# Small matmuls of a fused two-layer kernel, issued inside weight units instead of between them

## The reference

```python
mod = silu(c) @ w_ada + b_ada
shift_m, scale_m, gate_m, shift_f, scale_f, gate_f = split(mod, 6)
h = rmsnorm(x, g_mix_pre) * (1 + scale_m) + shift_m
z = h @ w_in                       # q, k, v, fl (8 columns), pool, conv, three gates
log_f = log_sigmoid(fl + b_f); cum_f = cumsum(log_f)
logits = q @ k.T * scale + cum_f[query] - cum_f[key]   # 8 heads of 64, causal, softmax, @ v
merged = gate0 * (attn @ wa) + gate1 * (pool @ wb) + gate2 * (conv @ wc)
x = x + gate_m * rmsnorm(merged @ w_out, g_mix_post)
h2 = rmsnorm(x, g_ff_pre) * (1 + scale_f) + shift_f
x = x + gate_f * rmsnorm(square(relu(h2 @ w_ff1)) @ w_ff2, g_ff_post)
```

## Time and profile before

| | |
|---|---|
| median of 3 executions | 855.65 us (854.88 to 856.12) |
| profiled execution | 856.08 us |
| span of its profile | 854.7 us |
| PE busy | 801.0 us (94%) |
| DVE, ACT, POOL busy | 561.3, 416.5, 82.3 us |
| mean granted clock of TensorE | 0.974 of full |

### The profile page before, as it was taken

How to read it: one execution, slowest core, us unless ns; L and a number is a source line. 1 busy time by engine, 2 the same in 40 slices (tenths; PEclk the granted TensorE clock), 3 DMA queues, 4 the chain that set the end, 5 groups by cost and what they waited for, 6 DMA issues and landing times.

```text
span 854.7 us, 12953 instructions
## 1 busy us (share of the span) xinstructions
PE 801.0 (94%) x5264; PEld 728.8 (85%) x5264; DVE 561.3 (66%) x761; ACT 416.5 (49%) x610; POOL 82.3 (10%) x129
## 2 busy tenths in 40 slices
PE   2989999999969999999999999899987999999995
PEld 2889998999859999999989998688876999999994
DVE  4775887859965655656665889757444665555663
ACT  4445356653446454435456477447534644444341
POOL 6200960001110000000001000011000100000000
PEclk9998999999988999999999999999999999999998
DMA  9968777867644555555556554446434365565641
GB/s 306 351 220 293 260 261 255 290 230 260 210 135 131 190 189 181 187 183 179 191 178 192 174 151 149 144 152 201 141 99 123 124 197 183 187 191 183 194 148 50
DMA packets 83323, 163.70 MB, mean 192 GB/s; under 512 B 5424, under 2 KB 13808, under 8 KB 83264
## 3 DMA queue, kind: packets, MB, share of 16 engines
q1 hardware_dynamic: 81344, 157.31, 56.7%
q10 hardware_dynamic: 1424, 4.81, 1.7%
q0 software_dynamic: 496, 0.76, 0.3%
HBM read 161.81 MB, written 1.05 MB: 191 GB/s over the span
## 4 chain that ended last, share of the span: by engine, by line
PE 83%; ACT 7%; DVE 6%; issue 2%; POOL 1%; DMA 1%; SPq 0%; ACTq 0%; DVEq 0%; POOLq 0%
PE bank L1630 25%; PE bank L1631 25%; PE bank L1632 25%; ACT hi_ring L461 2%; DVE lo_ring L865 2%; PE bank L1784 1%; DVE ada_acc L897 1%; PE bank L1669 1%; PE bank L1689 1%; PE bank L2089 1%; DVE x_residual L971 1%; DMA ada_ring<-in_w_ada 1%; ACT gates L516 1%; PE bank L1798 1%; PE bank L1788 1%
## 5 line engine op out<-in xcount | busy, mean ns | idle before, releaser
L865 DVE TENSOR_TENSOR lo_ring<-raw_ring,hi_ring 128x1024 fp32r<-128x1024 f32 x248 | 304.9, 1234 | 209.0 <-ACT hi_ring L461 208.3
L461 ACT CAST hi_ring<-raw_ring 128x1024 fp32r<-128x1024 f32 x248 | 258.9, 1049 | 325.2 <-PE bank L1632 311.3
L1630 PE MATMUL bank<-h_hi,hi_ring 128*128 128x256 f32 x1008 | 292.5, 290 | 1.5 <-DVE h_lo L930 1.5
L1631 PE MATMUL bank<-h_lo,hi_ring 128*128 128x256 f32 x1008 | 289.2, 287 | 0.0
L1632 PE MATMUL bank<-h_hi,lo_ring 128*128 128x256 f32 x1008 | 289.0, 287 | 0.0
L1630 PEld LDWEIGHTS bank<-h_hi,hi_ring 128*128 128x128 f32 x1008 | 197.7, 196 | 4.8 <-issue 3.2
L1631 PEld LDWEIGHTS bank<-h_lo,hi_ring 128*128 128x128 f32 x1008 | 197.8, 196 | 0.8 <-issue 0.2
L1632 PEld LDWEIGHTS bank<-h_hi,lo_ring 128*128 128x128 f32 x1008 | 197.5, 196 | 0.0
L1630 PE MATMUL bank<-hi_ring,branch_hi 128*128 128x512 f32 x320 | 125.7, 393 | 2.8 <-DVE branch_lo L1009 2.7
L1631 PE MATMUL bank<-lo_ring,branch_hi 128*128 128x512 f32 x320 | 124.7, 390 | 0.0
L1632 PE MATMUL bank<-hi_ring,branch_lo 128*128 128x512 f32 x320 | 124.5, 389 | 0.0
(11 more groups left out here) (259 smaller groups left out, 937.3 us busy)
## 6 DMA issues: line engine op xcount, KB each, us to landing
raw_ring<-in_w_ff SPq DMA_DIRECT2D x128, 512.0 KB, 3.7
raw_ring<-in_w_in SPq DMA_DIRECT2D x64, 512.0 KB, 4.3
raw_ring<-in_w_out SPq DMA_DIRECT2D x16, 512.0 KB, 3.5
raw_ring<-in_w_xkv SPq DMA_DIRECT2D x16, 512.0 KB, 3.7
mem_v<-in_w_ada SPq DMA_DIRECT2D x12, 512.0 KB, 5.8
ada_ring<-in_w_ada SPq DMA_DIRECT2D x10, 512.0 KB, 4.9
mem_k<-in_w_ada SPq DMA_DIRECT2D x10, 512.0 KB, 5.3
raw_ring<-in_w_branch SPq DMA_DIRECT2D x8, 512.0 KB, 5.1
```

Of the source, the lines that this page charges most:

```text
L461: act.copy(m.hi[:, m.slot(u)], m.raw[:, m.slot(u)]).then_inc(s.hi_done, 1)
L865: dve.tensor_tensor(m.lo[:, m.slot(u)], m.raw[:, m.slot(u)], as_f32(m.hi[:, m.slot(u)]), ALU.subtract).then_inc(s.lo_done, 1)
L1630: pe.matmul(out, a_hi, b_hi, start=start, stop=False, skip_group_check=True)
L1631: pe.matmul(out, a_hi, b_lo, start=False, stop=False, skip_group_check=True)
```

## The change

Three pieces of small work move from the gap between two units into a unit: `unit_features` and `unit_tokens` get a function `beside`, called after each tile of three passes.

- The forget logits go from behind unit 14 into unit 15, two of the 16 matmuls after each of its eight tiles. Bank 0, into which they go, is wanted by unit 16.
- The scores of the first attention go from behind the unit of their step into that unit, one of the four parts after each second tile (first, third, fifth and seventh).
- The shift's columns go from behind unit (c = 4, j = 1) into the next unit, one matmul after each of eight tiles. The scale's columns go from ahead of unit 52 into it, two after each of its four tiles. Each column now counts up its semaphore, so the readers wait for 8. DVE reads the shift two units later, and the scale after its split of unit 56 instead of before it.

```diff
-                dve.wait_ge(s.ff_shift_ps, 1)
+                dve.wait_ge(s.ff_shift_ps, 8)
...
-            if c == 4 and j == 1:
+            if c == 4 and j == 3:
                 ada_columns(s.ff_shift_ps, s.ff_shift, 0, 8, 16, 24)
...
-    ada_columns(s.ff_cols_ps, s.ff_cols, 6, 8, 24, 32, G_FF)
     for n in range(2):
         for j in range(RING):
             if j == RING - 1:
                 post_scale(s.post1, n, OUT_BANKS[n], m.rows[:, 0, :])
+            if n == 0 and j == 1:
+                ada_columns(s.ff_cols_ps, s.ff_cols, 6, 8, 24, 32, G_FF)
...
                 mm = three_passes(bank[banks[f // 2]][:, (f % 2) * S:(f % 2) * S + S], m.hi[:, slot, k, fc],
                                   m.lo[:, slot, k, fc], x_hi[:, k0 + k, :], x_lo[:, k0 + k, :],
                                   first and k == 0 and f % 2 == 0, last and k == UK - 1)
+                if beside:
+                    beside(tiles * k + f)
...
-    def forget_logits():
-        pe.wait_ge(s.q_out, 2)
-        pe.wait_ge(s.small_in, SMALL_LOADS * DMA)
-        for tt in range(NT):
-            for k in range(KD):
-                mm = pe.matmul(bank[0][:, tt * NH:tt * NH + NH], m.h_f32[:, k, tt * P:tt * P + P], m.w_fl[:, k, :],
-                               start=(k == 0), stop=(k == KD - 1))
-        mm.then_inc(s.fl_ps, 1)
-        free[0] = s.fl_out, 1
+    def forget_logits(i):
+
+        if i == 0:
+            claim(0)
+            pe.wait_ge(s.small_in, SMALL_LOADS * DMA)
+        tt = i // 4
+        for k in (2 * (i % 4), 2 * (i % 4) + 1):
+            mm = pe.matmul(bank[0][:, tt * NH:tt * NH + NH], m.h_f32[:, k, tt * P:tt * P + P], m.w_fl[:, k, :],
+                           start=(k == 0), stop=(k == KD - 1), skip_group_check=True)
+        if i == 7:
+            mm.then_inc(s.fl_ps, 1)
+            free[0] = s.fl_out, 1
...
-                features(u, q, m.h_hi, m.h_lo, 2 * i)
-            if u == 14:
-                forget_logits()
+                features(u, q, m.h_hi, m.h_lo, 2 * i, beside=forget_logits if u == 15 else None)
...
+        def beside(i):
+            if i == 0:
                 claim(4, 5)
...
+            if i % 2 == 0:
+                score(s.att1, g, (4, 5), True, i // 2)
...
+    def ff_shift(i):
+        if i == 0:
+            claim(0)
+            pe.wait_ge(s.ada_used, 32)
+        ada_column(2, 0, i, s.ff_shift_ps)
+        if i == 7:
+            free[0] = s.ff_shift, 1
+
+    def ff_cols(i):
+        if i == 0:
+            claim(6)
+            pe.wait_ge(s.ada_used, 40)
+        ada_column(0, 6, 2 * i, s.ff_cols_ps)
+        ada_column(0, 6, 2 * i + 1, s.ff_cols_ps)
+        if i == 3:
+            free[6] = s.ff_cols, 1
```

More of the change, by code:

```diff
@@ L1632, in three_passes, with unit_features @@
         return pe.matmul(out, a_lo, b_hi, start=False, stop=stop, skip_group_check=True)
-    def unit_features(u, k0, x_hi, x_lo, banks, first, last, tiles=4):
+    def unit_features(u, k0, x_hi, x_lo, banks, first, last, tiles=4, beside=None):
         pe.wait_ge(s.lo_done, u + 1)
@@ L1643, in unit_features, with unit_tokens @@
                                   first and k == 0 and f % 2 == 0, last and k == UK - 1)
+                if beside:
+                    beside(tiles * k + f)
         return mm
-    def unit_tokens(u, k0, x_hi, x_lo, outs, first, last, cols=slice(0, UN), start_first=True):
+    def unit_tokens(u, k0, x_hi, x_lo, outs, first, last, cols=slice(0, UN), start_first=True, beside=None):
         pe.wait_ge(s.lo_done, u + 1)
@@ L1684, in turn_x, with ada_column @@
                 transposes(turn, m.x, tt, range(n * KD // 2, (n + 1) * KD // 2))
+    def ada_column(slot, b, i, done):
+        pe.matmul(bank[b][:, i:i + 1], m.ada_acc[:, slot + i // 4, i % 4 * P:i % 4 * P + P], m.ones[:, 0:1], start=True,
+                  stop=True, skip_group_check=True).then_inc(done, 1)
     def ada_columns(slot, slabs, b):
@@ L1771, in pe_program, with score, scores @@
             else:
-                features(u, q, m.h_hi, m.h_lo, 2 * i)
-            if u == 14:
-                forget_logits()
+                features(u, q, m.h_hi, m.h_lo, 2 * i, beside=forget_logits if u == 15 else None)
+            if u == 13:
+                free[0] = free[1] = s.q_out, 2
     free[5] = s.v_sum, 4
     free[2] = free[3] = s.k_out, 2
-    free[1] = s.q_out, 2
     free[6] = free[7] = s.mixA_out, 2
[L1780 to L1791, removed]
+    def score(a, g, banks, forget, i):
+        e, tt, c0, c1 = parts()[i]
+        rows = slice(64 * e, 64 * e + 64)
+        b = bank[banks[e]]
+        mm = pe.matmul(b[:, c0:c1], m.qT[rows, g, tt * P:tt * P + P], m.kT[rows, g, 0:c1 - c0], start=True,
+                       stop=not forget, skip_group_check=True)
+        if forget:
+            head = 2 * g + e
+            mm = pe.matmul(b[:, c0:c1], m.pick[0:2 * NH, head:head + 1].to_broadcast([2 * NH, P]),
+                           m.key_sums[0:2 * NH, 0:c1 - c0], start=False, stop=True, skip_group_check=True)
+        if i == 3:
+            mm.then_inc(a.scores.sem, 1)
+            free[banks[0]] = free[banks[1]] = a.logits.at(g + 1)
+    def scores(a, g, banks):
+        for i in range(4):
+            score(a, g, banks, False, i)
     def turn_prob(a, g, banks, soft):
@@ L1814, in attend, with scores1 @@
         free[b] = a.br.at(g + 1)
[L1816 to L1820, removed]
+    def scores1(step):
+        if step not in ATT1_AT:
+            return None
+        g = ATT1_AT.index(step)
+        def beside(i):
+            if i == 0:
                 claim(4, 5)
@@ L1826, in attention1 @@
                     pe.wait_ge(s.pick_ok, 1)
-                scores(s.att1, g, (4, 5), True)
+            if i % 2 == 0:
+                score(s.att1, g, (4, 5), True, i // 2)
+        return beside
+    def ff_shift(i):
[11 more added lines that the diff above has]
+        ada_column(0, 6, 2 * i + 1, s.ff_cols_ps)
+        if i == 3:
+            free[6] = s.ff_cols, 1
+    def attention1(step):
+        if step == 0:
+            cumulative()
+        for g, at in enumerate(ATT1_AT):
             if step == at + 4:
@@ L1836, in pe_program @@
     for j in range(RING):
-        features(MIX_B + j, j, m.h_hi, m.h_lo, 0)
+        features(MIX_B + j, j, m.h_hi, m.h_lo, 0, beside=scores1(j))
         attention1(j)
@@ L1845, in pe_program @@
             i = RING * c + j
-            features(GATES + i, j, m.h_hi, m.h_lo, b0)
+            features(GATES + i, j, m.h_hi, m.h_lo, b0,
+                     beside=ff_shift if (c, j) == (4, 2) else scores1(RING + i))
             attention1(RING + i)
@@ L1851, in pe_program @@
                 free[0], free[1] = (s.gate_row, 1), (s.gate_row, 3)
[L1852 to L1856, removed]
             if i == 13:
@@ L1889, in pe_program @@
             pe.wait_ge(s.merged_lo, j + 1)
-            tokens(OUT + RING * n + j, UK * j, m.h_hi, m.h_lo, b0, j == 0, j == RING - 1)
+            tokens(OUT + RING * n + j, UK * j, m.h_hi, m.h_lo, b0, j == 0, j == RING - 1,
+                   beside=ff_cols if n == 0 and j == 0 else None)
             if n == 1 and j == 1:
@@ L1972, in scores2 @@
             pe.wait_ge(s.k2_out, 2)
-        scores(s.att2, g, pair_banks(g), False)
+        scores(s.att2, g, pair_banks(g))
     def turn2(g):
```

16 lines of the change are left out of this document (7 added, 9 removed).

## The result

| | before | after |
|---|---|---|
| median | 856.12 us (5 executions, 854.88 to 858.39) | 864.72 us (5, 863.05 to 866.39) |
| ratio, 95% interval | | 1.0097 (1.0080 to 1.0115) |
| profiled execution, span | 856.08, 854.7 us | 865.01, 863.7 us |
| mean granted clock | 0.974 | 0.978 |
| DVE, ACT, POOL busy | 561.3, 416.5, 82.3 us | 562.6, 416.2, 82.2 us |

The change makes the kernel 8.6 us slower. The forecast was 4.2 us faster, the range ended at 855.0: both are wrong. The profiled executions differ by 8.9 us.

The account below looks back on a forecast made before the run. TensorE, on 83% of the chain of waits, was taken as the bound. Terms 2.5 + 4.5 - 2.3 + 0.1 - 0.6 = 4.2 us off 855.65 gave 851.4 us; range 848.9 to 855.0 (8 in 10).

Parts of the forecast that it names:

- the one on the shift's columns: 16 records inside a unit instead of ahead of it, DVE's read two units later: covered, priced at 0.
- Forget logits: Units 14 to 17: full clock saves 3.07 us, a new wait takes 0.55, net 2.5 us.
- the wait on L1089: Ahead of unit 16, TensorE waits for DVE to empty the forget logits' bank: some 0.5 us.
- The mixed unit: Rival, 13%: unit 15, 32 small records among 24 weight matmuls, still lowers the clock; 3.07 us stay, 854.5 us.
- Scores: First attention: three low stretches vanish, 4.5 us saved, against 2.3 us for 12 added changes between weight matmuls and scores.
- A boundary: Each change between weight matmuls and scores costs TensorE 0.19 us; three more per pair of heads.
- Scale's columns: At unit 52: full clock only brings TensorE 2 us early to a wait for `h_lo`; gain 0.1 us.
- The slower rival: Rival, 9%: the clock does not follow these runs or their grouping; nothing gained, 2.9 us added, 858.5 us.
- Another engine takes the gain: Rival, 10%: without low stretches, loads or DVE's splits may come late by 1 to 2 us; 853 us.
- the two waits for the probabilities unchanged: Sign of being right: TensorE's two waits for the probabilities, 1.1 us in all, stay as they are.
- Later restarts: Low stretches from 250.02 and 663.10: the clock may come back later, 0.3 us each, 0.6 us lost.

Follow-up runs that it names:

- before's order: The changed kernel with all three parts put back at their old places, so TensorE and DVE run what they ran before; 856.47 and 855.16 us.
- The unbroken run inside unit 19: The changed kernel with the shift read one unit earlier and all four score parts in one run behind the unit's fifth tile; 853.09 us, ratio 0.9981.
- the first experiment: The changed kernel with DVE's read of the shift's columns one unit earlier (j = 2 instead of 3); 855.34 us, ratio 0.9990.
- the scores alone: The changed kernel with the forget logits and both sets of columns back at their old places; 854.69 us, ratio 0.9979.
- the late read: The kernel before, with only DVE's read of the shift's columns moved from j = 1 to j = 3; 868.62 us, ratio 1.0142.
- the fastest kernel: The changed kernel with scores in two runs of two parts, first product with v one step later, shift read ahead of unit's split; 849.41 us, ratio 0.9922.
- the forget logits alone: The changed kernel with the scores and both sets of columns back at their old places; 855.33 us, ratio 0.9984.
- the columns back: The changed kernel with scores in two runs of two parts, shift's and scale's columns and their reads back as before; 853.04 us, ratio 0.9959.

## Why the prediction was wrong

**The step that failed** is the one on the shift's columns: "DVE reads them two units later; its next use of that accumulator is in the split after unit 40, one unit further: covered." It looked at who writes `ada_acc`, and not at who else wants bank 0, the bank that the columns are summed into. The diff had it: `free[0] = s.ff_shift, 1`. The columns used to be read at j = 1, when nothing claims bank 0 until unit 40; with the read at j = 3 DVE's step stands in the queue behind a split that ACT can only prepare 3.7 us after unit 39 has ended (178.9 to 182.66), at the very unit that claims the bank. Priced at 0, it was 7.1 us of wait and 2.2 us of low clock with it. The prediction had itself asked what is queued behind a waiting instruction for the forget logits, and did not ask it here.

**Right, nearly to the tenth:**

- Forget logits: 2.5 us net forecast, 16.70 - 14.12 = 2.58 measured; the wait on L1089 was 0.33, not 0.5. The mixed unit kept the clock at 1.00 in all eight executions that had it.
- Scores: step 3, 9 and 21 forecast 0.92 each (1.49 - 3 x 0.19), measured 0.96, 0.93, 1.06. Step 15, which had no low stretch, forecast +0.57, measured +0.56. These are single profiles: by the executions of before's order step 9 or 15 could have come out the other way round. A boundary, here the first part of step 3 after (the distance from the last L1633 to L1798 and from the first L1631 to L1632, as in the earlier trace rows):

```profile
90.14 0.28 PE L1633 MATMUL bank<-h_hi,lo_ring 128*128 128x256 f32 x1
90.35 0.49 PE L1798 MATMUL bank<-k_T,q_T 64*128 64x128 f32 x2
...
91.01 0.38 PE L1631 MATMUL bank<-h_hi,hi_ring 128*128 128x256 f32 x1
91.23 0.28 PE L1632 MATMUL bank<-h_lo,hi_ring 128*128 128x256 f32 x1
```

  0.21 and 0.22, as before: the boundary costs the same inside a unit. The Trainium skill (TensorEngine Tiling (Array Packing), Key Properties) says that a change of tiling mode drains TensorE. The trace fits that at the entry alone (0.21 instead of 0.12): at the exit, have 0.20 behind one-column matmuls of 128 rows too, where the mode does not change, so most of the 0.22 has another cause.
- Scale's columns: forecast 0.1. Units 41 to 54 gain 0.78, but 0.73 of it is the wait at unit 41 that the loss at unit 40 had taken, so 0.05; the low stretch was hidden by `h_lo`, as forecast. Not forecast was that half clock can follow that wait itself: it did in three of the six executions with these columns inside unit 52, at about 1.6 us (the row 54 to 56).
- Before 184 the clock followed the unbroken runs of small matmuls: where they were broken up, no low stretch was left in this or the other profiles. (The prediction counts four of five such runs with a low stretch behind them; its own rows show five of six.) The slower rival said that it would not, and so that nothing would be gained; 5.0 us were (2.58 and 2.39). That rival had the sign and none of the steps: the loss came from elsewhere. The Trainium skill (TensorE: Matmul & The Clock Gate, Part 1) names gaps of idle TensorE as what brings the throttle back. For the 184.20 stretch the trace agrees, since it begins inside a wait. Of the five, the first four began with no gap between TensorE's records, so by the records no idle time brought them. But "busy" is modelled, and a small record of 0.112 us holds 8 columns or 1, so whether the engine counts as idle inside such a run the profile cannot say; the trace does not settle it.

**Wrong in size:**

- "Another engine takes the gain" stood at 10% with 1 to 2 us, and it is what happens at unit 24, beside everything else; the sign "the two waits for the probabilities unchanged" failed there. TensorE waits 1.7 us for DVE's copy of the probabilities (L1004). DVE by the timeline after:

```profile
108.34 1.63 DVE L897 SCALAR_TENSOR_TENSOR ada_acc<-mem_k,silu_c,ada_acc 128x1024 f32<-128x1024 f32 x1
109.89 1.76 DVE L865 TENSOR_TENSOR lo_ring<-raw_ring,hi_ring 128x1024 fp32r<-128x1024 f32 x1
111.57 1.76 DVE L897 SCALAR_TENSOR_TENSOR ada_acc<-mem_v,silu_c,ada_acc 128x1024 f32<-128x1024 f32 x1
113.26 0.54 DVE L1004 COPY prob_T<-bank 128x384 f32<-128x384 f32 x1
```

  Its two operations per unit take 1.63 to 1.76 us each here, 1.22 to 1.28 at unit 40, so 3.4 us for a unit that TensorE does in 2.88. The earlier trace rows average this away: 78% over 100 us holds a stretch in which DVE is full. POOL works on pooling and convolution in that stretch. In this trace both operations take 1.21 to 1.28 us each time from 124 to 212, where POOL is idle, and between 80 and 230 the longer ones stand only where POOL works; that POOL is what slows them was not tried.

  Three things make the 1.7 us, by unit 24 to 25 in the executions. The low stretch behind step 3 had let DVE catch up: 4.18 with it and 4.84 without, in the two executions of before's order (0.66). The forget logits inside unit 15 alone give 4.46 (0.28). And the scores inside unit 19 give 5.69 without a low stretch, 0.85 over 4.84. Together they make 1.79, against 1.72 measured. The unbroken run inside unit 19 has its low stretch and gives 5.23, against 5.89 in pieces: 0.66 again. For 0.7 of the 0.85 the timeline of DVE has a reason, first in before's order (scores from 95.85 on, unit 20 from 99.05), then with the scores inside (unit 20 from 99.33):

```profile
96.97 0.68 DVE L935 COPY mix<-bank 128x512 f32<-128x512 f32 x1
99.16 1.39 DVE L982 SCALAR_TENSOR_TENSOR softmax<-bank,cum_log_f,mask 128x128 f32<-128x128 f32 x4 [1.51 <-PE bank L1804]
```
```profile
99.53 0.69 DVE L935 COPY mix<-bank 128x512 f32<-128x512 f32 x1 [2.85 <-PE bank L1632]
100.14 1.38 DVE L982 SCALAR_TENSOR_TENSOR softmax<-bank,cum_log_f,mask 128x128 f32<-128x128 f32 x4
```

  DVE copies an accumulator of unit 19 ahead of the softmax. With the scores behind the unit it does so beside them; with the scores inside, unit 19 and its scores end together, and the softmax starts 0.81 us behind the start of unit 20 instead of 0.11. The prediction compared the chains of ACT and TensorE from the end of the next unit and not DVE's.
- "Later restarts", 0.6 us forecast, were 2.1 us in the first experiment (-0.36 at unit 60, +1.65 and +0.80 in the last two rows of the table), 3.5 when it was run again and 2.0 in the change. Unit 60 to 61 alone takes 2.94 to 5.26 us over the thirteen profiles, with before's 4.57 on the slow side. The larger part is the number of low stretches: one near 620 appears in both executions of the earlier read, in the scores alone, the late read, the change and the fastest kernel, and in none of the three executions of before's order, the forget logits alone, or the other three. Where it stands TensorE has an idle gap and small matmuls of the cross attention in all versions. What decides whether the clock falls there stays open: it is neither the order of instructions near it, which is the same in all, nor the shift of its start alone, which is 3.4 us both in the first experiment and with the columns back, the one with and the other without.

Had the read been placed right, the forecast 851.4 would still have been 4 us low (855.34). By its profile, which gains 0.5 us from unit 14 on, 3.7 are missing: 1.7 at unit 24, 0.3 for the first probabilities just ahead of it (units 21 to 24), and 1.5 by the late low stretches beyond the forecast; the rest are differences of under 0.3 us.

## What to carry to other kernels

When a step of one engine is moved later in its program, list everything that its signal releases, accumulators first, and look up in the trace what stands in front of it in its new place; a step of 0.16 us cost 9 us here because it was put behind a wait of another chain. Work out a gain on TensorE against the busiest neighbour in the same ten microseconds, not against its mean over a hundred. And where short matmuls of another kind must run among full ones, put them in as few runs as keep the clock: two runs of 1.6 us (first to third part, 91.43 to 93.03 in the unbroken run) did in the three executions that have them, one of 3.2 us did not always, four cost 0.37 us more per pair. And read more than one profile before listing where the clock is low.

## What was not expected of the hardware

- A run of 1.8 us of one-column matmuls (16 records) lowered the granted clock for 3.4 us with TensorE busy by its records all through that stretch, behind unit 37 (171.7, with a run of scores 0.8 us ahead of it) and ahead of unit 52 (219.4). The same run ahead of unit 52 left it at 1.00 in the two executions of the old order, and in those of the late read, of the forget logits alone and of the scores alone.
- The same program showed its low stretches at different places in different executions (75.0, 98.9, 122.8, 174.0 in one, 76.2, 147.9, 171.8 in another) while its time changed by 1.3 us. A mean clock of 0.978 after against 0.974 before, with 9 us more time, says nothing by itself: the clock was higher, and the time went into a wait.
- The wait of 7 us brought low clock both times, from within it: for 6.84 us in the change, 10.2 with the late read alone. It cost 2.2 and 2.4 us more on unit 40, so such a wait is not priced by its length alone.
